# A hybrid attention and expert step on one core: samples' second attention inside the prompt's loop, block-diagonal compressed values, seven pairs of weight buffers and low parts on VectorE

## What is computed

```python
z = x @ w_in                                  # q, k, v of two mixers, gates
o_a = stick_breaking(q_a, ...)                # 8 heads
# second mixer, for each query: three branches, each with its own softmax
o_b = g[..., 0:1] * o_c + g[..., 1:2] * o_s + g[..., 2:3] * o_w
m = concat(rms_norm(o_a) * g_A, rms_norm(o_b) * g_B) @ w_out
h = layer_norm(ALPHA * x + m)
y = layer_norm(ALPHA * h + peer(h))           # 16384 experts, 16 per head
```

## Time and profile before

| | us |
|---|---|
| median of 3 runs | 1099.77 |
| lowest, highest | 1098.5, 1102.85 |
| the profiled execution | 1107.55 |
| span in the trace | 1105.9 |
| TensorE busy | 1066.5 |
| VectorE busy | 856.9 |
| ScalarE busy | 555.2 |
| GpSimd busy | 137.8 |

### The profile page before, as it was taken

One profiled execution on the slowest core, in us unless ns is written; L12 is line 12 of the kernel. 1 busy time (PEld: TensorE's weight loads), 2 busy tenths in 40 slices (PEclk: granted clock), 3 DMA queues, 4 the chain that ended last, 5 costly groups with the idle time before them and its releaser, 6 DMA issues.

```text
span 1105.9 us, 23553 instructions
## 1 busy us (share of the span) xinstructions
PE 1066.5 (96%) x7256; PEld 954.3 (86%) x7256; DVE 856.9 (77%) x1950; ACT 555.2 (50%) x1057; POOL 137.8 (12%) x153
## 2 busy tenths in 40 slices
PE   6999989889999999999999999999999999999996
PEld 6997645879999999999999999998788888888875
DVE  4324353788988888887658999978888888888877
ACT  4435454544453544443554555545555555555543
POOL 0244401100001000454100000001010101010100
PEclk9999986989999999999999999999999999999998
DMA  7655903243458866899974444458888888888872
GB/s 252 259 204 185 350 39 115 84 145 115 139 186 276 272 236 230 310 409 392 319 249 140 139 140 143 142 165 276 319 284 296 281 294 286 296 286 289 293 236 90
DMA packets 96248, 253.19 MB, mean 229 GB/s; under 512 B 11424, under 2 KB 44224, under 8 KB 95408
## 3 DMA queue, kind: packets, MB, share of 16 engines
q1 hardware_dynamic: 81840, 196.84, 51.5%
q0 software_dynamic: 14368, 55.87, 14.4%
HBM read 232.60 MB, written 22.12 MB: 230 GB/s over the span
## 4 chain that ended last, share of the span: by engine, by line
PE 85%; DMA 7%; DVE 4%; ACT 2%; issue 1%; SPq 0%; DVEq 0%; ACTq 0%
PE ps L541 13%; PE ps L542 13%; PE ps L543 12%; PE ps L993 10%; PE ps L995 10%; PE ps L994 10%; DMA activations<-u_out 6%; PE ps L966 5%; PE ps L625 1%; DVE w_lo L1358 1%; PE ps L897 1%; PE ps L772 1%; DMA a_in<-activations 1%; PE ps L980 1%; PE ps L769 0%
## 5 line engine op out<-in xcount | busy, mean ns | idle before, releaser
L1358 DVE TENSOR_TENSOR w_lo<-ring,w_hi 128x512 fp32r<-128x512 f32 (+1 forms) x458 | 389.5, 853 | 137.7 <-ACT w_hi L1041 124.1
L1041 ACT CAST w_hi<-ring 128x512 fp32r<-128x512 f32 (+1 forms) x460 | 345.8, 752 | 98.7 <-PE ps L995 62.5
L541 PE MATMUL ps<-h_hi,w_hi 128*128 128x256 f32 (+1 forms) x1128 | 330.6, 293 | 3.0 <-DVE w_lo L1358 3.0
L542 PE MATMUL ps<-h_lo,w_hi 128*128 128x256 f32 (+1 forms) x1128 | 321.0, 285 | 0.0
L543 PE MATMUL ps<-h_hi,w_lo 128*128 128x256 f32 (+1 forms) x1128 | 319.3, 283 | 0.0
L541 PEld LDWEIGHTS ps<-h_hi,w_hi 128*128 128x128 f32 x1128 | 214.9, 191 | 7.0 <-issue 3.9
L542 PEld LDWEIGHTS ps<-h_lo,w_hi 128*128 128x128 f32 x1128 | 214.2, 190 | 0.0
L543 PEld LDWEIGHTS ps<-h_hi,w_lo 128*128 128x128 f32 x1128 | 211.8, 188 | 0.0
L993 PE MATMUL ps<-w_hi,y_hi 128*128 128x512 f32 x512 | 199.8, 390 | 0.7 <-DVE y_lo L1823 0.5
L994 PE MATMUL ps<-w_hi,y_lo 128*128 128x512 f32 x512 | 199.2, 389 | 0.0
L995 PE MATMUL ps<-w_lo,y_hi 128*128 128x512 f32 x512 | 199.2, 389 | 0.0
(11 more groups left out here) (349 smaller groups left out, 1274.9 us busy)
## 6 DMA issues: line engine op xcount, KB each, us to landing
ring<-in_uT_dram SPq DMA_DIRECT2D x128, 512.0 KB, 3.6
ring<-in_v_dram SPq DMA_DIRECT2D x128, 512.0 KB, 4.4
activations<-u_out SPq DMA_DIRECT2D x128, 128.0 KB, 3.3
a_in<-activations SPq DMA_DIRECT2D x128, 128.0 KB, 4.2
ring<-in_w_in_dram SPq DMA_DIRECT2D x22, 512.0 KB, 4.4
ring<-in_w_q_dram SPq DMA_DIRECT2D x16, 512.0 KB, 3.2
ks<-in_cache_sb_dram POOLq DMA_DIRECT2D x16, 256.0 KB, 3.2
vs<-in_cache_sb_dram POOLq DMA_DIRECT2D x16, 256.0 KB, 5.4
```

Of the source, the lines that this page charges most:

```text
L541: mm(out, hi, hi_, start=start, stop=False)
L542: mm(out, hi, lo_, start=False, stop=False)
L1041: nc.scalar.copy(w_hi[slot][:, x], ring[:, ring_slot, x]).then_inc(part_hi, 2 if half is None else 1)
L1358: V.tensor_tensor(w_lo[slot][:, x], ring[:, ring_slot, x], w_hi[slot][:, x].bitcast(F32), ALU.subtract).then_inc(part_lo[ring_slot], 2 if ...
```

## The change

It has these parts.

- The samples' second attention moves into the loop. Its ten transposes stand at `u == 7` ahead of the last `np_turn`, the first sum of squares behind that, its values at `u == 8` ahead of the last `np_values`; they use other PSUM banks. ScalarE exponentiates it in two portions, at `u` 2 and 3. `ss_tokens` moves from `u == 6` to `u == 5`.
- `sc_` holds both groups' compressed probabilities side by side, 32 columns apart, so that one transpose of 47 columns takes both, once per pair of units. Their values `cvd` are block-diagonal (47 rows, 128 columns, zeros from GpSimd), so that one product does both groups. The second unit of a pair has neither.
- VectorE's order in the loop: `ss_argument` ahead of `np_max(2)`, `np_out` and `ss_picked` ahead of `np_max`, `np_scale(u + 1)` in turn `u`.
- A seventh pair of buffers for `w_hi` and `w_lo`, of which the output projection uses five (`OUT_PLACE`), and eight different banks (`OUT_BANK`).
- GpSimd's four low parts go to VectorE. Three squares of four become one instruction (128x1152), and sums take two planes at once (128x576). The second sum of squares stands behind four half tiles instead of two.
- The layer norm has its own rows for sums, variance and deviation, and one low part stands ahead of `stretch`.

```diff
+        OUT_PLACE = (2, 3, 6, 0, 1, 6, 0, 1)
+        OUT_BANK = (4, 5, 7, 6, 0, 1, 2, 3)
...
@@ gpsimd
+            nc.gpsimd.memset(cvd[:, :], 0.0)
+            nc.gpsimd.memset(sc_[:, :, 0, NC_:32], 0.0).then_inc(cmp_clear, 1)
...
-            for n in range(AT_OUT, AT_OUT + 4):
-                slot = n % 4
-                pool.wait_ge(part_hi, 2 * (n + 1))
-                nc.gpsimd.tensor_tensor(w_lo[slot][:, :], ring[:, slot, :], w_hi[slot][:, :].bitcast(F32),
-                                        ALU.subtract).then_inc(part_lo[slot], 2)
...
@@ tensor, np_turn and np_values
-                for tt in range(2):
-                    ins = nc.tensor.transpose(ps[0:NC_, 4 + tt, 384:512], sc_[:, 8 * (u % 2) + u // 2 * 2 + tt, :], ident)
-                ins.then_inc(np_t, 1)
+                if u % 2 == 0:
+                    for tt in range(2):
+                        both = sc_[:, u + tt, :, :].rearrange("p g n -> p (g n)")[:, 0:32 + NC_]
+                        ins = nc.tensor.transpose(ps[0:32 + NC_, 4 + tt, 384:512], both, ident)
+                    ins.then_inc(np_t, 1)
...
-                mm(ps[halves_[br], 6, 0:256], cv[:, 0, halves_[br]], ptc[:, br, :], start=br == 0, stop=False)
+                if br == 0:
+                    mm(ps[:, 6, 0:256], cvd[:, :], ptc[:, :], start=True, stop=False)
...
@@ tensor, the loop and the projection
             for u in range(9):
                 if u + 2 < 8:
                     np_scores(u + 2)
+                if u == 7:
+                    ns_turn()
                 if u < 8:
                     np_turn(u)
+                if u == 7:
+                    rms_sums(0)
+                if u == 8:
+                    ns_values()
                 if u >= 1:
                     np_values(u - 1)
...
-            first_tiles(range(2), range(4))
+            out_tile(0, range(4))
+            out_tile(1, range(4))
+            out_tile(2, range(4))
+            pe.wait_ge(np_o, 4)
+            out_tile(3, range(4))
             rms_sums(1)
-            first_tiles(range(2, 4), range(4))
-            first_tiles(range(4), range(4, KD))
+            for c in range(4):
+                out_tile(c, range(4, KD))
             for c in range(4, KD):
-                pe.wait_ge(m_pre, c - 3)
-                project(place(AT_OUT + c), o_parts, c, halves(0, AT_OUT + c))
+                out_tile(c, range(KD))
...
@@ scalar, the end of the loop
-                if u >= 6:
-                    high_of(AT_OUT + u - 6)
+                if u == 7:
+                    act.wait_ge(ns_tb, 1)
+                    nc.scalar.copy(ptss[:, :, :], ps[:, 2:4, :])
+                    nc.scalar.copy(ptns[:, :, :], ps[0:32, 0, :].rearrange("p (a b) -> p a b", b=256))
+                    nc.scalar.copy(ptcs[:, :], ps[0:NC_, 1, 0:256]).then_inc(ns_pt, 1)
                 np_copy(u)
...
+                if u == 6:
+                    act.wait_ge(ss_o, 1)
+                    A(sqb[:, 0:4, :], oT[:, 0:4, :], ACT.Square).then_inc(rm_sq, 1)
+                    high_of(AT_OUT)
+                    high_of(AT_OUT + 1)
...
@@ scalar, when the later tiles' high parts are made
-                high_of(n + 4, 2 * AT_OUT + 4 + c + 1 if c < 4 else 2 * (n + 1))
+            before = (None, OUT_DONE[2], OUT_DONE[3], OUT_DONE[4], OUT_DONE[0], OUT_DONE[1], OUT_DONE[6], OUT_DONE[7])
+                high_of(AT_OUT + 4 + c, before[c])
                 act.wait_ge(m_pre, c + 1)
...
@@ vector, the loop
+            np_scale(0)
+            ss_argument()
+            for u in range(8):
+                if u in (3, 5, 7):
+                    np_out((u - 3) // 2)
+                if u == 3:
+                    ss_picked(0)
+                if u == 5:
+                    ss_picked(1)
+                if u == 6:
+                    dve.wait_ge(ss_tok, 1)
+                    V.tensor_copy(oT[:, 0:4, TP:T], ps[:, 7, 0:128].rearrange("p (h t) -> p h t", h=4)).then_inc(ss_o, 1)
+                if u + 2 < 8:
+                    np_max(u + 2)
+                if u + 1 < 8:
+                    np_scale(u + 1)
+                if u == 1:
+                    ns_maxima()
+                if u == 4:
+                    ns_scale()
 
             squares_added(0)
+            low_next()
+            low_next()
...
@@ vector, the residual
+            for c in range(4):
+                residual(c)
+            dve.wait_ge(m_pre, 4)
+            link(V.tensor_tensor(sum2[:, :, :], xTs[:, 0:2, :], xTs[:, 2:4, :], ALU.add))
+            low_next()
+            residual(4)
+            dve.wait_ge(ln_sq, 4)
+            link(V.tensor_tensor(squ2[:, :, :], sqb[:, 0:2, :], sqb[:, 2:4, :], ALU.add))
+            low_next()
+            low_next()
+            residual(5)
...
@@ vector, ahead of the layer norm's last step
+            center(1)
+            low_next()
             dve.wait_ge(ln_sd, 2)
```

302 lines of the change are left out of this document (145 added, 157 removed).

## The result

The changed kernel took 1094.77 us, median of 7 executions (1093.57 to 1098.28), beside 1102.85 for the kernel before on the same chip: 0.9937 of its time, 95% interval 0.9916 to 0.9959, or 4.5 to 9.3 us faster. I had forecast 1087.5 us, in a range from 1084 to 1094.5, and a gain of 12.3 us, 1.1%. The kernel is faster, by about half of what I said.

The account below looks back on a forecast made before the run. It took TensorE, busy 1066.5 of 1105.9 us, as the bound, with waits and half speed costing time; 2.2 + 11.8 - 1.6 = 12.4 us off 1107.55 gave 1095.2, less 7.8 gave 1087.4, stated as 1087.5, range 1084 to 1094.5.

Parts of the forecast that it names:

- it lies 7.8 above the median, 1099.77, for which I assume the same difference: Whole kernel, last step: the traced execution's distance from the median carries over, turning 1095.2 us into 1087.4.
- the sum: Whole kernel: gains and losses of four parts of TensorE's path, 12.4 us off the profiled 1107.55, giving 1095.2.
- stretch 2: Unit-7 key scores to end of last two transposes (169.40 to 198.51): 11.8 us gained, about 7 from half speed.
- stretch 3: Last transposes to last tile's residual (198.51 to 229.99), the output projection: 1.6 us lost, from 0 to 4.
- Stretch 1: Loop up to unit 7's key scores (169.40): 2.2 us gained, from 0.5 to 3.
- the reason that I gave for the fall: Loop and projection, 140 to 240 us: TensorE's waits bring the half speed behind them, so a wait costs twice.
- over 34 was my sign of being wrong: Last transposes to last residual: more than 34 us there would show the forecast wrong.
- the wait for the second sum of squares: Output projection, ahead of the second halves: TensorE waits about 2.5 us, with 0.8 added for another clock fall.
- Stretch 4: Last residual to first query product (to 236.17): 0.5 us gained and 0.5 lost, so 0.
- The long fall at the loop's end: Rival, loop's end: the clock falls again, gain 6 us, 1093.8 us; chance 0.15.
- The projection waited more than I had counted: Rival, output projection: full clock fall costs 3.2 us, waits could be 1 more, 1091.5 us; chance 0.12.
- The early wait: Rival, near 144 us: `ss_argument` lengthens the wait, half speed lasts 18 us instead of 8, 1091 us; chance 0.05.

Follow-up runs that it names:

- group 1: Timed executions taken together: kernel before, 23 executions, median 1102.51 us; changed kernel unedited, 12 executions, 1096.42 us, ratio 0.9951; three edited versions too.
- before_again: Kernel before, unedited, run once more for a second trace; traced span 1102.3 us.
- before_twin: Kernel before, unedited, traced and timed against itself as if it were a change; 1102.46 us, ratio 0.9993.
- before_order: Kernel before with only VectorE's copies ahead of the maxima, `ss_argument` first, and `ss_tokens` one unit earlier; 1105.57 us, ratio 1.0027.
- comp_twice: Changed kernel with the compressed transposes and a compressed value product put back into the odd units; 1098.53 us, ratio 0.9956 to before.
- sq_first: Changed kernel with ScalarE squaring the residual ahead of the high part from tile 3 on; 1095.93 us, ratio 0.9946 to before.
- mended: Changed kernel, second sum of squares ahead of tile 3, squares ahead of high parts, tile 6's low part ahead of `residual(4)`; 1092.66 us, ratio 0.9912 to before.
- arg_late: Changed kernel with `ss_argument` back behind `np_max(2)`, nothing else; 1092.88 us, ratio 0.9917 to before.
- order_vec: Kernel before with VectorE's and the tokens' order of the change, and VectorE making GpSimd's first four low parts; 1095.35 us, ratio 0.9925.
- rms_early: Changed kernel with the second sum of squares ahead of the first half of tile 3; 1094.53 us, ratio 0.9926 to before.

## Why the prediction was wrong, point by point

**The step that failed is the last: "it lies 7.8 above the median, 1099.77, for which I assume the same difference".** I took 7.8 us off the 1095.2 that the sum gave for a traced execution, and the changed kernel's medians are not 7.8 below its traced executions but 0 and 3 us above them (1094.77 and 1094.77; 1096.42 and 1093.5). The 7.8 belonged to two samples of the kernel before and not to the kernel: over the 100 executions of it that are listed the median is 1103.4 (1094.3 to 1109.7), the traced execution of 1107.55 lay 4.2 above that, and the median of three, 1099.77, 3.6 below.

What made the traced execution slow can be told in part. Its mean clock was 0.982, 40 us at half clock (2 × 0.018 × 1107.55); the executions timed have 30 to 35. About 7 of the 11.8 us of stretch 2 were half speed that would not come. But over many executions the change moved the half-clock time from 33 to 29 us (group 1), which is worth 2 us and not 6 (7 less the 0.8 of stretch 3). Some of what it saved from 174 to 192 it gave back in the layer norm, whose fall grew to 10.2 us, and in one of two traces behind the early wait, 10.2 us against 6.8. Where in the quicker executions of before the half-clock time is missing stays open.

**That the traced execution took 1094.77 where the sum gave 1095.2 is luck.** The stage gained 9.75 us of the 12.4; the other 3.0 came from behind it, where the change does nothing (869.7 us from the first query product to the end before, 866.7 changed). There TensorE waits for low parts, and the view of waits from 480 to 740 us gives for before, and then for before_again,

```profile
PE ps L541 <- DVE w_lo L1358: 3.0, 4, 0.9
```

```profile
PE ps L541 <- DVE w_lo L1358: 0.2, 1, 0.2
```

with 2.1 us in before_twin and 5.3 in before_order, kernels whose code is the same there.

**The mechanism was right in size and in part in its reason.** Stretch 1: 1.6 and 2.2 us gained in the two traced pairs (scores 7 at 167.7 and 167.0 against 169.3 and 169.2), forecast 2.2. The removed products cost what their rows say (comp_twice), the block-diagonal one 0.63 us and not 0.43, and the longer wait 0.55 us (2.22 less 1.67) and not 0.75. Stretch 2: 16.9 us in both traces of the changed kernel against 29.2, so 12.2 gained, forecast 11.8; the clock stayed at 1.00 and `ss_tokens` took 1.96 us. But the reason that I gave for the fall, the waits ahead of it, is not borne out: before_order has none of them and has the fall.

**Stretch 3 was mis-sized.** Forecast 1.6 us lost, measured 3.4 and 2.5 (34.8 and 33.9 against 31.4); over 34 was my sign of being wrong, and one of the two traces has it. I had the wait for the second sum of squares (2.58, forecast 2.55) and the fall behind it (3.4 us; my 3.7 is not what the 0.66 of the earlier trace rows gives, which is 3.4 as well). I had the last residual over 1 us behind the last tile, but not the transfer that ScalarE's order puts ahead of a square: VectorE's 10.2 us of work were counted without any wait in them, and there were 1.05 us at 207.8 and 0.71 at 217.0. sq_first took 1 to 1.9 us of this stretch away. **Stretch 4**, forecast 0, lost 0.7: the product of ones ran at half clock (1.34 us in the chain, 0.75 in mended).

**The rivals.** The long fall at the loop's end did not come in either trace of the changed kernel. The projection waited more than I had counted: this rival, given 0.12, is what happened to the stage, at 9.75 to 11.4 us instead of 12.4, though by VectorE's waits and not by the full fall of clock that I priced. The early wait grew from 1.67 to 2.22 us; the ratios of arg_late put the price of the early `ss_argument` at 2.2 us (0.9917 against 0.9937) to 3.7 (against 0.9951), not resolved by the intervals, where I had 0.75. It seems to make the fall behind it longer and more frequent. "Each fall follows waits of TensorE", which I read from the earlier trace rows, is false as a rule: a wait of the same length had a fall behind it or not, and before_order's fall had no wait ahead of it.

**Where the gain is.** order_vec, with VectorE's order, the tokens and the low parts alone, reaches 0.9925, a whole change's gain within the intervals. The rest (samples' attention inside the loop, block-diagonal values, another order of the tiles) gains 4 to 5 us more up to the transposes' end and loses 6.5 to 7.4 in the projection (34.8 or 33.9 against 27.4 us). With the edits of mended it loses 2.3.

## What to carry to other kernels

Before a change is priced, look at the mean clock of every execution that is listed, not only of the traced one: where they spread, the half speed seen in one trace need not be that of the median execution, and the distance of one traced execution from the median belongs to that execution: it is no term that can be carried over to the changed kernel. When a product waits for a small chain on other engines (a sum of squares), put it into the queue where its input becomes ready, and not behind the work that is to hide it. And when an order on VectorE is moved, look what GpSimd does at the new time: an order that fills TensorE's waits gained nothing until GpSimd's low parts were out of its way (before_order, order_vec).

## What was not expected of the hardware

The granted clock fell to its lower level with TensorE busy all the time: from 166 to 176 us in before_order (rows above), and in rms_early and sq_first, in that order, where the windows show it busy 6.00 of 6 us:

```profile
172.00:178.00 6.00, 6.00 (x42) 4.80 (x42) 3.06 (x10) 3.96 (x6) 0.00 (x0) 0.72 0.53 183
```

```profile
172.00:178.00 6.00, 6.00 (x42) 4.79 (x42) 2.97 (x10) 3.93 (x7) 0.00 (x0) 0.72 0.42 166
```

What TensorE did 0.2 us (rms_early, sq_first) and 1.4 us (before_order) ahead of these falls was the eight products of 16 columns each (`ss_tokens`, 1.96 us in all three), but the same products at the same place had no fall behind them in ten other traces; the cause stays open. And the same wait at 142 to 145 us (1.67 and 1.68) was followed by a window of 147 to 155 at 0.57 or at 1.00 in two executions of the kernel before.

VectorE's scalings, each with one input in SBUF and a scalar for each partition, stood still beside GpSimd's low parts: 5.14 us for 1.01 of work. The Trainium skill, "SBUF — State Buffer", section "Who interferes with whom", says that VectorE and GpSimd take a shared pair of ports by a lock that is held for a whole instruction, and that a VectorE instruction with one SBUF input is free of it unless it runs in a two-port mode. The trace agrees with the lock (a scaling that begins inside a low part ends 0.08 us behind it, twice) and shows that these in-place scalings fall under it.
